# Gated attention pairs of a two-block transformer kernel: output laid out by feature, with reciprocals turned on TensorE

## The reference

```
proj = h @ w_in                                   # fq, fk, fv (8 heads of 64), gate, dq, dk, dv
log_f = log_sigmoid(fgate + fox_forget_b)         # (tokens, 8)
c = cumsum(log_f)                                 # one decay row per head
fox_o  = attention(fq, fk, fv, decay=c)           # logits q.k/8 + c[t] - c[s], causal, softmax, @ v
diff_o = rms_norm(attention(q1,k1,v) - lam*attention(q2,k2,v)) * 0.8     # 4 heads of 128
out = concat([fox_o, diff_o]) @ w_out
```

## Time and profile before

| what | value |
|---|---|
| runs | 995.57, 992.7 and 996.19 us, median 995.57 us |
| span of the profiled execution | 990.5 us, 14542 instructions |
| PE busy | 986.0 us (100%) |
| DVE, ACT, POOL busy | 711.5, 486.3 and 213.1 us |
| fox pairs on PE, from the scores of pair 4 to the fox half of the output product | 268.89 to 301.93 us of the span |

### The profile page before, as it was taken

One profiled execution on the slowest core, in us unless ns is written; L12 is line 12 of the kernel. 1 busy time (PEld: TensorE's weight loads), 2 busy tenths in 40 slices (PEclk: granted clock), 3 DMA queues, 4 the chain that ended last, 5 costly groups with the idle time before them and its releaser, 6 DMA issues.

```text
span 990.5 us, 14542 instructions
## 1 busy us (share of the span) xinstructions
PE 986.0 (100%) x5302; PEld 835.5 (84%) x5302; DVE 711.5 (72%) x849; ACT 486.3 (49%) x621; POOL 213.1 (22%) x215
## 2 busy tenths in 40 slices
PE   9999999999999999999999999999999999999998
PEld 6888888888888888888888888888888888888887
DVE  6766666775788767676777998678875767667674
ACT  6534343664666543434545444365555445334342
POOL 3313232014100232323112600060000012223230
PEclk9999999999999999999999999999999999999999
DMA  9665656745425656565745625544536456556561
GB/s 316 224 212 169 212 169 214 253 131 190 129 85 170 209 173 210 171 205 177 247 154 174 204 94 200 188 145 147 168 121 220 130 184 230 172 178 201 179 210 42
DMA packets 121017, 178.53 MB, mean 180 GB/s; under 512 B 5760, under 2 KB 82112, under 8 KB 120848
## 3 DMA queue, kind: packets, MB, share of 16 engines
q1 hardware_dynamic: 120048, 174.86, 53.8%
q0 software_dynamic: 576, 1.39, 0.5%
q10 hardware_dynamic: 352, 1.73, 0.5%
HBM read 176.88 MB, written 2.64 MB: 181 GB/s over the span
## 4 chain that ended last, share of the span: by engine, by line
PE 99%; DMA 0%; SPq 0%; ACT 0%; issue 0%; DVE 0%
PE acc L662 11%; PE acc L666 10%; PE acc L665 10%; PE tp L863 10%; PE gu L863 10%; PE gu L868 5%; PE tp L868 5%; PE tp L662 4%; PE tp L666 4%; PE tp L665 4%; PE gu L662 3%; PE gu L665 3%; PE gu L666 3%; PE acc L1143 2%; PE acc L1146 1%; PE acc L1172 1%
## 5 line engine op out<-in xcount | busy, mean ns | idle before, releaser
L2002 DVE TENSOR_TENSOR wlo<-raw,whi 128x2048 fp32r<-128x2048 f32 x140 | 325.7, 2331 | 153.9 <-ACT whi L1363 152.4
L1363 ACT ACTIVATE whi<-raw 128x2048 fp32r<-128x2048 f32 x150 | 285.7, 1908 | 70.3 <-PE acc L666 22.7
L863 PE MATMUL tp<-act_in,whi 128*128 128x512 f32 x432 | 102.9, 390 | 0.0
L863 PE MATMUL gu<-act_in,whi 128*128 128x512 f32 x432 | 102.6, 390 | 0.0
L1899 POOL TENSOR_TENSOR tmp<-tmp 128x256 f32<-128x256 f32 x54 | 39.7, 736 | 275.8 <-DVE tmp L2123 275.8
L1901 POOL TENSOR_TENSOR sil<-sil,tmp 128x256 f32<-128x256 f32 x54 | 88.8, 1644 | 33.5 <-ACT sil L1434 33.5
L863 PEld LDWEIGHTS gu<-act_in,whi 128*128 128x128 f32 x432 | 80.9, 188 | 16.6
L662 PE MATMUL acc<-whi,hT_hi 128*128 128x512 f32 x240 | 94.0, 392 | 0.0
L665 PE MATMUL acc<-wlo,hT_hi 128*128 128x512 f32 x240 | 93.7, 390 | 0.0
L666 PE MATMUL acc<-whi,hT_lo 128*128 128x512 f32 x240 | 93.4, 389 | 0.0
L863 PEld LDWEIGHTS tp<-act_in,whi 128*128 128x128 f32 x432 | 79.8, 188 | 15.7
(11 more groups left out here) (379 smaller groups left out, 1845.8 us busy)
## 6 DMA issues: line engine op xcount, KB each, us to landing
raw<-in_w_in SPq DMA_DIRECT2D x96, 512.0 KB, 4.7
raw<-in_down SPq DMA_DIRECT2D x66, 512.0 KB, 4.1
raw<-in_gate SPq DMA_DIRECT2D x64, 512.0 KB, 4.4
raw<-in_up SPq DMA_DIRECT2D x64, 512.0 KB, 4.9
raw<-in_w_out SPq DMA_DIRECT2D x16, 512.0 KB, 4.7
raw<-in_w_branch_hg SPq DMA_DIRECT2D x8, 512.0 KB, 4.3
raw<-in_w_branch_attn SPq DMA_DIRECT2D x8, 512.0 KB, 4.8
post<-in_post_gains SPq DMA_DIRECT2D x3, 512.0 KB, 6.2
```

Of the source, the lines that this page charges most:

```text
L863: pe.matmul(banks[:, a, :], w_hi[:, i, a * P:(a + 1) * P], both, start=i == 0, stop=False)
L1363: act.activation(split_weights(k)[0], raw[:, k % RING, :], ACT.Copy).then_inc(hi_ready, 1)
L2002: dve.tensor_tensor(w_lo, raw[:, k % RING, :], w_hi.bitcast(F32), ALU.subtract).then_inc(lo_ready, 1)
```

## The change

Fox pairs only; pairs 0 to 3 and 8 to 11 keep their work.

- Scores: both heads as 64 rows each (rows 0 to 63 and 64 to 127) into a bank of its own for each head. q and k are one copy each. The decay comes in through extra bf16 matmuls over 6 rows (three bf16 parts of each decay and three ones), which lie at rows 0 and 64 of a tile of their own. POOL splits the decay rows into three parts before it sends them through DRAM.
- Reciprocals: DVE takes the reciprocals with each of the four row sums repeated 64 times, 128x256 elements; PE turns them in two further transposes of 128x128, behind the six squares.
- Values: v (64 columns) is the stationary operand and a turned square of 128 columns moves; the two heads go to rows 0 to 63 and 64 to 127 of the output. One DVE multiplication by the turned reciprocals of 128x256 takes the place of the four scalings. The result is already turned, so ACT rounds it into `act_hi` (`fox_hi`) and DVE takes the rest (`fox_lo`), and the two fills with their DVE and ACT steps are gone.
- Order: `FOX_BEHIND` of pairs 4 and 5 is (2, 1). `weights_out` copies 512 columns on each of ACT and DVE. `values` waits for both copies in every pair. `maxima` of pairs 5 and 6 is no longer split around `k_out`. `hi(N_WOUT + 3)` stands behind `weights_out(7)`.

```
-FOX_BEHIND = {4: (1, 2), 5: (1, 2), 6: (1, 1), 7: (0, 0)}
+FOX_BEHIND = {4: (2, 1), 5: (2, 1), 6: (1, 1), 7: (0, 0)}
...
+            return score_banks(p)[:, h, 0:S] if p < 8 else late(p)[:, h * S:(h + 1) * S]
...
+        def fox_place(p):
+            return score_banks(p)[:, :, 3 * P:4 * P]
+        fox_pT = proj[:, :, FOX_WEIGHTS:FOX_WEIGHTS + BLK]
+        def fox_rden(p):
+            return proj[:, p % 2, MIX:MIX + S]
+        def fox_scaled(p):
+            return heads(dec_sb[:, p % 2, 0:S], 2)
...
+                if kind < 2:
                     at = [slice(64 * h, 64 * h + 64) for h in range(2)]
...
+                    if kind == 0:
+                        decay = [slice(64 * h, 64 * h + AUG) for h in range(2)]
+                        for h in range(2):
+                            pe.matmul(late_half(p, h), aug_q[decay[h], i, P:S], aug_k[decay[h], i, :], start=False,
+                                      stop=False, skip_group_check=True)
+                        for h in range(2):
+                            pe.matmul(early_half(p, h), aug_q[decay[h], i, 0:P], aug_k[decay[h], i, 0:P], start=False,
+                                      stop=False, skip_group_check=True)
...
+                if pair(p)[0] == 0:
+                    pe.wait_ge(exp_done, p + 1)
+                    for h in range(2):
+                        for n in range(3):
+                            to = (n + 1) % 3 * P
+                            pe.transpose(turned[:, h, to:to + P], e_sb[:, h, n * P:(n + 1) * P], idn)
+                    pe.wait_ge(rden_ready, p + 1)
+                    for t in range(TT):
+                        mm = pe.transpose(turned[:, t, 3 * P:4 * P], fox_rden(p)[:, (1 - t) * P:(2 - t) * P], idn)
+                    mm.then_inc(pT_full, 1)
...
+                    for h in range(2):
+                        pe.matmul(o[at[h], 0, :], v[0][:, at[h]], fox_pT[:, h, 0:P], start=True, stop=True,
+                                  skip_group_check=True)
...
-            pe.wait_ge(o_out, 8)
-            fills(T_WOUT, from_proj(MIX), 2, 3)
             half(N_WOUT + 1, 0, wout_banks(1), 1, 1, first_j=1)
-            filled(T_WOUT, 3)
+            pe.wait_ge(fox_lo_ready, 3)
+            half(N_WOUT + 2, 0, wout_banks(0), 0, 0, tiles=[0, 1, 2], first_j=1)
+            pe.wait_ge(fox_lo_ready, 4)
...
+            def fox_hi(p):
+                act.wait_ge(o_out, p + 1)
+                act.activation(heads(act_hi[:, p - 4, :], 2), fox_scaled(p), ACT.Copy).then_inc(fox_hi_ready, 1)
...
+            def fox_reciprocals(p):
+                dve.wait_ge(exp_done, p + 1)
+                dve.reciprocal(heads(fox_rden(p), 4), per(den[:, :], 64)).then_inc(rden_ready, 1)
...
+                    dve.tensor_tensor(fox_scaled(p), fox_place(p), fox_pT[:, :, 3 * P:4 * P], ALU.mult).then_inc(o_out, 1)
```

The order on DVE in `diff_and_fox`, after the scores of pair 4, with the lines added and taken out:

```
                 fill_scaled(T_WOUT, 1)
+                fox_reciprocals(4)
                 half_lo(N_WOUT, 1)
                 block_out(N_WIN, 0, 23)
                 fill_rest(T_WOUT, 0)
                 weights_out(4)
-                late_maxima(5)
+                maxima(5)
                 k_out(6)
-                maxima(5, late_found=True)
                 output(4)
                 fill_rest(T_WOUT, 1)
+                fox_reciprocals(5)
                 half_lo(N_WOUT + 1, 0)
                 weights_out(5)
-                late_maxima(6)
+                maxima(6)
                 k_out(7)
-                maxima(6, late_found=True)
                 output(5)
+                fox_lo(4)
+                fox_reciprocals(6)
                 half_lo(N_WOUT + 1, 1)
-                reciprocals(6)
                 maxima(7)
                 weights_out(6)
                 output(6)
+                fox_lo(5)
+                fox_reciprocals(7)
                 half_lo(N_WOUT + 2, 0)
                 weights_out(7)
+                fox_lo(6)
+                output(7)
                 half_lo(N_WOUT + 2, 1)
-                output(7)
+                fox_lo(7)
```

More of the change, by code:

```diff
@@ L62 @@
 BY_TILE, BY_HALF = [(0, 0), (0, 1), (1, 0), (1, 1)], [(0, 0), (1, 0), (0, 1), (1, 1)]
-DIFF_FIRST = [(0, 1), (1, 1), (0, 0), (1, 0)]
-FILLS = [DIFF_FIRST if u == T_WOUT else BY_HALF if u in (T_FFN1, T_WOUT2) else BY_TILE for u in range(9)]
+DIFF_ONLY = [(0, 1), (1, 1)]
+FILLS = [DIFF_ONLY if u == T_WOUT else BY_HALF if u in (T_FFN1, T_WOUT2) else BY_TILE for u in range(9)]
 C_ID, C_TRI, C_ONES, C_MASK, C_COS, C_SIN, C_SAME = 0, 128, 256, 384, 512, 528, 544
@@ L447, in turn_n @@
         def turn_n(u):
[L448 removed]
+            return 4 * u - (4 if u > T_WAT else 0) - (2 if u > T_WOUT else 0)
         def stationary(u, t, j, a):
@@ L984, in scores @@
                 for h in range(2):
[L985 to L997, removed]
+                    q, k = q_sb[:, h, :], k_sb[:, h, :]
+                    pe.matmul(late_half(p, h), q[:, P:S], k, start=True, stop=True)
+                    mm = pe.matmul(early_half(p, h), q[:, 0:P], k[:, 0:P], start=True, stop=True)
                 mm.then_inc(scores_done, 1)
@@ L1547, in weights_out @@
                     act.wait_ge(pv_done, p)
-                n = S if pair(p)[0] == 1 else 3 * P
-                act.activation(pT_sb[:, 0, 0:n], turned[:, 0, 0:n], ACT.Copy).then_inc(pT_a, 1)
+                n = (4 * P, S, 3 * P)[pair(p)[0]]
+                to = pT_sb if pair(p)[0] else fox_pT
+                act.activation(to[:, 0, 0:n], turned[:, 0, 0:n], ACT.Copy).then_inc(pT_a, 1)
             def diff_and_fox():
@@ L1611, in diff_and_fox @@
                         exps(p + 1)
+                    else:
+                        hi(N_WOUT + 3)
                     if p == 4:
                         next_hi(N_WIN, 0, 23)
+                    fox_hi(p)
             def rounded_out(p):
@@ L1725, in _ @@
             diff_and_fox()
-            hi(N_WOUT + 3)
-            fills(T_WOUT, 2, 3)
             hi(N_FFN2)
@@ L2211, in k_out, with maxima @@
                        .then_inc(kT_ready, 1)
[L2213 to L2219 removed]
+            def maxima(p):
                 dve.wait_ge(scores_done, p + 1)
@@ L2250, in weights_out @@
                     return
-                dve.tensor_copy(pT_sb[:, 1, :], turned[:, 1, 0:3 * P]).then_inc(pT_d, 1)
-                if pair(p)[0] == 0 and p != 6:
-                    reciprocals(p)
+                to, n = (pT_sb, 3 * P) if pair(p)[0] else (fox_pT, 4 * P)
+                dve.tensor_copy(to[:, 1, 0:n], turned[:, 1, 0:n]).then_inc(pT_d, 1)
             def late_reciprocals(p):
```

142 lines of the change are left out of this document (69 added, 73 removed).

## The result

The changed kernel takes **996.07 us** (median of 13 runs, 995.59 to 998.9). The kernel before, run beside it 13 times, has a median of 995.27 (992.59 to 996.25). The ratio is **1.0023, 95% interval 1.0012 to 1.0033**: a small loss, clear of 1 but under the bound of 0.5%. On this chip the runs of the kernel before fell into two groups, 992.6 to 992.9 and 995.3 to 996.3; no span or clock is listed for them, so what parts them is open. On the chips of the experiments it took 992.4 to 992.6 as a median, and the changed kernel 996.08, so the change costs **3.5 us** there, ratio 1.0036 (1.0023 to 1.005, run changed_again), where I had forecast 5.2.

What follows compares the result with a forecast made beforehand. PE was taken to set the pace, DVE 0.54 us per pair behind. PE's -2.1, -0.1 and waits of 7.5 us gave +5.3, or +5.2 from the measured start; on 995.57 that made 1000.8 us, range 996.3 to 1002.8.

Steps and rivals of the forecast that it cites:

- The mechanism: Pairs 4 to 7: DVE's wide reciprocals stand ahead of work PE needs, so PE waits, together 7.5 us.
- the walk: PE, DVE and ACT queues stepped through pairs 4 to 7 up to the fox half, good to 0.2 us: +5.3 us.
- 2.19 from start to start: DVE's reciprocal of 128x256 per pair, from a line through 2, 4 and 8 elements; taken as 2.2 us.
- slow, but partly covered (a smaller slope beyond 8 elements): Rival: reciprocal of 1.5 to 1.9 us, waits partly covered, +2.5 to +4.1 us, about 999; chance 0.20.
- PE's terms: Per pair scores -0.06, weights +0.22, values -0.47 us; fills -0.87 once; PE sum -2.1 us.
- The sum's lower bound: Lowest value given for the sum of PE's changes: -2.9 us, beside an upper bound of +0.3.
- my upper bound: Scores per pair: +0.08 us at worst, if the six-row matmuls run one after the other with a further late start.
- Nothing later is late: Behind pair 7: next stage's weight parts end 0.9 us before PE is at the last units' first half; loads come earlier.
- The order (2, 1) decides none: Units of pairs 4 and 5: the order removes PE's 0.20 us wait for the copies and nothing else.
- A quick reciprocal: Rival: reciprocal as quick as a copy, 0.42 us; -1.2 us, 994.4 us; chance 0.12.
- The base: Time the forecast change was added to: 995.57 us, the median of the runs, with a span of 990.5.
- the signs: Expected: 2.2 us reciprocals, DVE nearly never idle from 275 to 305, PE waits of 1 to 2 us, fox half about 307.

Runs made afterwards that it cites:

- changed_again: The changed kernel, unedited, run again beside the kernel before on the chip of the variants: 996.08 us, ratio 1.0036.
- recip_copy: Changed kernel with the reciprocal taken of 128x4 elements and one copy spreading it over 128x256: 992.56 us, ratio 1.0002 to the kernel before.
- sweep: Kernel with copied reciprocals, plus reciprocals and scalar multiplications of 8 to 512 elements appended at the end: 1014.49 us, not compared.
- changed_lo2_early: Changed kernel, wide reciprocal kept, with half_lo(N_WOUT + 2, 1) moved ahead of fox_lo(6) and output(7): 995.22 us, ratio 1.0028 to the kernel before.
- order_1_2: Changed kernel with the old unit order, (1, 2) for pairs 4 and 5: 996.06 us, ratio 1.0036 to the kernel before.
- best_1_2: Changed kernel with copied reciprocals, half_lo(N_WOUT + 2, 1) earlier, half_lo(N_WOUT + 1, 1) later, and old unit order (1, 2): 991.59 us, ratio 0.9993 to the kernel before.
- recip_twice: Changed kernel with each wide reciprocal done twice, one behind the other: 1005.99 us, ratio 1.0135 to the kernel before.
- before_2_1: Kernel before with the unit order (2, 1) for pairs 4 and 5 alone: 993.46 us, ratio 1.0011 to the kernel before.

## Why the prediction was off, step by step

- **The mechanism was right.** The wide reciprocal is in the open, and its replacement by a small one takes away all of the loss (recip_copy). The waits stand where the walk put them: behind DVE's work in pair 4, at the last transposes of pairs 5 to 7, at values(6).
- **The size of one term was wrong**: "2.19 from start to start" is 1.67. I drew a line through widths of 2, 4 and 8, where a constant is most of the duration: 35 ns between two rows carry the slope. The sweep has 6.25 ns per element and 0.15 us, where I had 8.3 and 0.136. Four times 0.53 us is 2.1 us. The walk with 1.67 gives +3.2 for my +5.2 (between its recorded values for 1.6 and 2.0 us), with waits of 0.5, 0.6, 0.4, 0.6, 1.9 and 1.3 us. It ends at the fox half. There the traces have +2.4 at the full clock (changed_again) and +2.7, with waits of 0.9, 0.2, 0.3, 1.8 and 1.1 us: 1 us less waiting than in the walk. The stretch to x measures +3.0 and the medians +3.5. So the closeness of +3.2 to them is partly luck: the tail, which the walk had at nothing, adds 0.65 or 0.2. The outcome is the rival "slow, but partly covered (a smaller slope beyond 8 elements)", at +2.5 to +4.1, that I gave 0.20.
- **PE's terms held.** Scores 1.44 us (1.46 forecast), the sum -2.3 (-2.1, above). Values take 0.80 from their first start; my 0.79 had the late start of 0.09 in it, with which they take 0.89. (The sum's lower bound should have read -3.0: 4 x (-0.19 + 0.22 - 0.57) - 0.87.) The Trainium skill (TensorEngine Tiling (Array Packing), section Key Properties) says that a change of tiling mode drains TensorE. Had six rows been another mode than 64, scores would have come near 1.6 by my upper bound; the six-row matmuls took 0.27 us for four, and no further late start stands in front of them: from the matmuls ahead (L993) to them it is 0.32 us, as from the same matmuls to the mask in the diff pairs. So nothing of that kind shows here.
- **"Nothing later is late" was wrong.** I compared the time when the last weight parts are ready, not the one when SP may ask for the piece behind. The request went out 6.3 us later than before, and 2.8 us later against the start of the fox half. In the changed kernel that costs 0.9 us by the medians and 0.6 by the tail (changed_lo2_early), and it hides 1.25 us of recip_copy's gain. My walk to the fox half at 307 (it was at 305.4) could not see it, as it ended ahead of it.
- **"The order (2, 1) decides none" came out in the changed kernel** (order_1_2, 996.06 against 996.08), but by luck, as 0.7 us in the fox part and 0.7 in the tail cancel. By itself it was wrong: +1.05 us on the kernel before, and probably 0.6 to 0.8 us in favour once DVE is quick (best_1_2, on another chip). The wait for `output` suggests that the order and the single `output` operation belong together.
- **A quick reciprocal** would have made the change worth -1.2 us by my rival. The same theory with a copy came to 992.56, +0.15, and to 991.31, -1.1, with the late load mended: so the rival's sum came out but for that load, though PE waited 0.8 us before values(6) where it had 1.1.
- **The base was the larger miss.** I put the sum on 995.57, the median of three runs of which one (992.7) stood 3 us below the others. In every run whose span is listed the time is 1.8 to 2.0 us above the span, so the trace that I read, with its 990.5 us, is that of an execution of about 992.3 us (an estimate), in the lower of the two groups. The 5.1 us between span and median that I noted were the sign of it. Of the 4.7 us between 1000.8 and 996.1, the base is 3.0 and the reciprocal 2.0; the 0.3 by which +3.5 exceeds +3.2 goes the other way. The changed kernel comes to 996.1 on either chip, and that is +3.5 from 992.6 but +0.8 from 995.3. With this base even the right sum, +3.2, would have given 998.8, inside the range that the measured time missed. The range's low end should have been worked out from the lower of the two levels.

Of the signs, the waits came at the places told, if shorter. The reciprocals took 1.75 us and not 2.2, and DVE idled for some 4 us between 275 and 305, where I had it nearly without idle time.

What stays open: the two groups of the kernel before; 0.3 to 0.5 us between the stretch's +3.0 and the medians' +3.5 (scores(4) starts 0.2 to 1.0 us later in all other traces than in the one of before, in before_2_1 too, so this may be the scatter of the start); and the 3 us of recip_twice beyond its waits.

## What to carry to other kernels

Don't take the slope of an operation from its smallest tiles, where a constant is most of the time: look for one wide row, or keep the far ends in the range. If a value must be repeated across many elements, do the slow operation on the small tile and let a copy spread it (0.42 us for 1.67). When a step is moved behind one that needs another engine, ask of each buffer that it frees who asks for the next load there, and follow that load to its first user.

## What the runs showed of the hardware that I had not expected

- DVE's reciprocal of float32 takes 0.15 us and 6.25 ns per element, from 8 to 512 elements, also with a repeated input; multiplication by a constant takes 0.29 us at 256 and 0.43 at 512.
- A copy that spreads the 4 values of `rden` over 256 elements took 0.29 us, where the copy of 256 elements from `acc` takes 0.42.
- After the same wait of 1.72 us before values(6), one execution was granted less than the full clock for some 3.9 us (down to 1.2 GHz) and another all of it; the stretch to x takes 44.83 and 44.88 us. In recip_twice PE is at 1.2 GHz in two stretches of 5.6 and 9.0 us and busy for 5.6 and 7.6 of them, so there the clock very likely costs time; no run separates it.
